# The values product of the first attention from rounded parts: the turned block copied by VectorE, rounded by ScalarE, its rest formed by GpSimd

## The chip, the cores and the metric

The kernel runs on one core of a Trainium2 chip. The metric is the device time of one execution in microseconds (us). Three runs of the kernel before took 2088.79, 2089.62 and 2090.61 us; the median is 2089.62 us. TensorE is PE in the profile, VectorE is DVE, ScalarE is ACT, GpSimd is POOL, and SyncE, which issues the weight loads, is SP.

## What is computed

The whole program is two transformer layers (an attention layer and a gated linear attention layer, each with an MLP) and a third layer with three mixers, for 512 tokens of width 1024. The change lies in the first layer's attention alone:

```python
s = jnp.einsum('bqhgd,bkhd->bhgqk', qblk, k, preferred_element_type=jnp.float32) * scale
p = jax.nn.softmax(s, axis=-1).astype(v.dtype)
return jnp.einsum('bhgqk,bkhd->bqhgd', p, v)
```

There are 16 query heads of width 64, 4 key/value heads, 512 tokens, no mask, float32 throughout.

## The kernel before

Activations lie transposed: 128 partitions are features, 512 columns are tokens. Almost every product is made from rounded parts. A float32 operand is split into `hi`, its value rounded to the type `float32r` (fp32r in the profile), and `lo`, the rest; `three` (lines 253 to 257) adds hi x hi, hi x lo and lo x hi into one PSUM bank by three matmuls. For weights ScalarE makes `w_hi` and VectorE `w_lo`.

The first attention (`attn_pe`, `attn_act`, `attn_dve`, `attn_pool`, lines 549 to 818) has two parts. First six blocks of the QKV projection are multiplied, while ScalarE and VectorE normalise and rotate queries and keys. Then comes a loop over `NU` = 64 units. Unit u is query tile u % 4 (128 queries) of head u // 4. Each engine has its own instruction queue, worked off in order, and its own loop over steps s; a unit passes through the engines with a fixed lag in steps, written out by hand:

- `scores(u)`, PE, step u: two matmuls against the keys' two parts, into bank 4 + u % 4.
- `top(u)`, DVE, step u + 2, for even u only: one reduction over the banks of units u and u + 1 gives both negated row maxima (`a_nmax`).
- `probs(u)`, ACT, step u + 2: exp of the scores with that bias, into one of four slots of `trow` (tile `sq`).
- `turn(u)`, PE, step u + 3: four 128x128 transposes into bank 2 + u % 2.
- `turned(u)`, DVE, step u + 4: one copy of that bank to `p_turned`, which holds two heads and lies where `h_hi` lies.
- `values(u)`, PE, step u + `A_LAG`, `A_LAG` = 8: one float32 matmul `a_v` x `p_turned`, accumulated over the four key chunks of head u // 4. The profile shows it as two records (x128 for 64). Half of `a_v`'s columns are ones, so that the product also gives the sum of the probabilities. The chunk 0 of a head waits for all four copies of the head.
- `inverse(h)`, ACT, once per head: logarithm and exp of the sums. `normed(h)`, DVE: multiply by it. `out_hi`, ACT, and the subtraction at line 818, POOL, once per two heads: the two parts of the output `a_q2` for the next projection.

Between these stand, once each, the rotation of the last query block (`evacuate`, `root`, `q_hi` on ACT; `cosine`, `sine`, `rotated`, `rooted`, `low` on DVE) and a weight block split in quarters. The output projection (`project`) follows: two of its eight row tiles at step 67, five behind the loop, the last in `pe_proj`.

The waits are on semaphores. The one that pairs DVE and ACT stands in `top` and `probs`:

```python
            def probs(u):
                act.wait_ge(a_top, u // 2 + 1)
                if u >= 4:
                    act.wait_ge(a_T, u - 3)
```

## Time and profile before

| | us |
|---|---|
| median of three runs (2088.79 to 2090.61) | 2089.62 |
| profiled execution, its time | 2088.29 |
| its span | 2086.6 |
| PE busy | 2029.9 (97%) |
| PE weight loads busy | 1629.5 (78%) |
| DVE busy | 1120.7 (54%) |
| ACT busy | 746.2 (36%) |
| POOL busy | 551.4 (26%) |

The profiled execution's own time is 1.7 us more than its span, and 1.3 us below the median of the runs. The attention loop lies between 94 and 216 us of the span. Rows of the timeline give the start of an instruction, its duration, engine, line, operation, names and shape. Durations of neighbours on one engine overlap a little, since an instruction starts before the record of the one ahead has ended; from start to start is what an engine needs for one.

### The profile page before, as it was taken

What the parts mean: (1) busy time and instruction counts of PE and PEld (TensorE: products, weight loads), DVE (VectorE), ACT (ScalarE), POOL (GpSimd) and SP (SyncE); (2) the same over time, 40 slices, a digit from 0 to 9 for tenths busy, and PEclk for the clock granted to TensorE, in tenths of its full rate; (3) what the DMA queues carried; (4) which work ended last, traced back from release to release, by engine and by line L of the source; (5) the groups of instructions that cost most, each with busy time, mean ns of one, the idle gap of its engine ahead of it and who ended that gap; (6) DMA issues with size and microseconds to landing.
All of it is one profiled execution on the core that took longest, in us unless ns stands there. A gap on an engine that the chain in (4) does not pass through costs nothing.

```text
span 2086.6 us, 23886 instructions
## 1 busy us (share of the span) xinstructions
PE 2029.9 (97%) x9416; PEld 1629.5 (78%) x9416; DVE 1120.7 (54%) x1127; ACT 746.2 (36%) x792; POOL 551.4 (26%) x497
## 2 busy tenths in 40 slices
PE   7999999999999998999999999999999989999996
PEld 5766778888877987778888888788988858888885
DVE  4697345455464435445555555783334464545455
ACT  5566332222234433322222234445553242222322
POOL 1100299990000000189991001423310000000000
PEclk9999999999999999999999999999999999999998
DMA  5400144433312220153442222232133312222221
GB/s 186 132 21 1 65 157 162 161 121 101 101 61 104 71 99 34 41 181 142 161 141 81 101 81 89 76 83 66 57 101 101 101 41 101 101 84 100 98 101 41
DMA packets 31773, 200.44 MB, mean 96 GB/s; under 512 B 3632, under 2 KB 3760, under 8 KB 8912
## 3 DMA queue, kind: packets, MB, share of 16 engines
q1 hardware_dynamic: 25552, 168.44, 23.5%
q0 software_dynamic: 6144, 30.94, 4.6%
q8 instruction: 53, 0.87, 0.2%
q14 instruction: 24, 0.20, 0.0%
HBM read 191.50 MB, written 2.10 MB: 93 GB/s over the span
## 4 chain that ended last, share of the span: by engine, by line
PE 95%; DVE 2%; ACT 2%; issue 1%; DMA 0%; DVEq 0%; SPq 0%; ACTq 0%
PE ps L255 26%; PE ps L257 26%; PE ps L256 25%; PE ps L612 3%; PE ps L367 2%; PE ps L599 1%; PE ps L1505 1%; PE ps L286 1%; PE ps L288 1%; PE ps L287 1%; PE ps L1050 1%; PE ps L1309 1%; PE ps L587 1%; PE ps L588 1%; PE ps L1489 1%
## 5 line engine op out<-in xcount | busy, mean ns | idle before, releaser
L217 ACT ACTIVATE w_hi<-w_raw 128x2048 fp32r<-128x2048 f32 x144 | 275.7, 1915 | 706.9 <-PE ps L257 706.7
L225 DVE TENSOR_TENSOR w_lo<-w_raw,w_hi 128x2048 fp32r<-128x2048 f32 x140 | 324.3, 2317 | 198.1 <-ACT w_hi L217 196.5
L255 PE MATMUL ps<-h_hi,w_hi 128*128 128x512 f32 x944 | 379.1, 402 | 7.9 <-DVE h_lo L419 4.0
L256 PE MATMUL ps<-h_lo,w_hi 128*128 128x512 f32 x944 | 371.1, 393 | 0.0
L257 PE MATMUL ps<-h_hi,w_lo 128*128 128x512 f32 x944 | 370.9, 393 | 0.0
L377 POOL TENSOR_TENSOR sq<-sq 128x1024 f32<-128x1024 f32 x9 | 31.6, 3509 | 879.4 <-ACT sq L351 729.4
L1293 POOL TENSOR_SCALAR ada_t<-ada_w,prm 128x256 f32<-128x256 f32 x192 | 220.2, 1147 | 9.9 <-DMA ada_w<-in_ada 9.0
L255 PEld LDWEIGHTS ps<-h_hi,w_hi 128*128 128x128 f32 x944 | 179.5, 190 | 51.5 <-issue 15.7
L257 PEld LDWEIGHTS ps<-h_hi,w_lo 128*128 128x128 f32 x944 | 179.1, 190 | 38.6
L256 PEld LDWEIGHTS ps<-h_lo,w_hi 128*128 128x128 f32 x944 | 179.4, 190 | 37.0 <-issue 1.4
L914 DVE TENSOR_TENSOR x<-x,ps 128x1024 f32<-128x1024 f32 x128 | 155.8, 1217 | 90.7 <-PE ps L257 90.7
L255 PE MATMUL ps<-m_xhi,w_hi 128*128 128x512 f32 x512 | 204.1, 399 | 0.0
L257 PE MATMUL ps<-m_hi,w_lo 128*128 128x512 f32 x512 | 203.0, 397 | 0.0
L257 PE MATMUL ps<-m_xhi,w_lo 128*128 128x512 f32 x512 | 203.0, 396 | 0.0
L255 PE MATMUL ps<-m_hi,w_hi 128*128 128x512 f32 x512 | 202.7, 396 | 0.0
L256 PE MATMUL ps<-m_xlo,w_hi 128*128 128x512 f32 x512 | 201.2, 393 | 0.0
L256 PE MATMUL ps<-m_lo,w_hi 128*128 128x512 f32 x512 | 201.2, 393 | 0.0
L1300 POOL TENSOR_TENSOR ada_acc<-ada_acc,ada_t 128x256 f32<-128x256 f32 x168 | 160.4, 954 | 14.0
L924 DVE SCALAR_TENSOR_TENSOR m_r<-ps,rstd 128x1024 f32<-128x1024 f32 x32 | 39.2, 1225 | 218.4 <-PE ps L257 218.4
L256 PEld LDWEIGHTS ps<-m_xlo,w_hi 128*128 128x128 f32 x512 | 96.2, 188 | 24.9 <-issue 1.0
L256 PEld LDWEIGHTS ps<-m_lo,w_hi 128*128 128x128 f32 x512 | 96.1, 188 | 23.9
L257 PEld LDWEIGHTS ps<-m_hi,w_lo 128*128 128x128 f32 x512 | 96.1, 188 | 23.5
(296 smaller groups left out, 3217.0 us busy)
## 6 DMA issues: line engine op xcount, KB each, us to landing
w_raw<-in_wb SPq DMA_DIRECT2D x154, 1024.0 KB, 4.9
ada_w<-in_ada POOLq DMA_DIRECT2D x24, 1024.0 KB, 5.4
a_sw<-a_g POOLq DMA_DIRECT2D x20, 128.0 KB, 2.8
x<-in_xT SPq DMA_DIRECT2D x4, 512.0 KB, 5.6
out_T<-x SPq DMA_DIRECT2D x4, 512.0 KB, 2.8
b_k<-b_k POOLq DMA_DIRECT2D x4, 256.0 KB, 5.4
b_kl<-b_kl POOLq DMA_DIRECT2D x4, 256.0 KB, 6.5
con<-in_con SPq DMA_DIRECT2D x1, 640.0 KB, 11.8
```

What stands on the lines that cost most here:

```text
L217: act.activation(w_hi[:, slot], w_raw[:, slot], ACT.Copy).then_inc(hi_done, 1)
L225: dve.tensor_tensor(w_lo[:, slot], w_raw[:, slot], w_hi[:, slot].bitcast(F32), ALU.subtract).then_inc(split_done, 1)
L255: pe.matmul(out, w[0], h[0], start=start, stop=False)
L256: pe.matmul(out, w[0], h[1], start=False, stop=False)
L257: return pe.matmul(out, w[1], h[0], start=False, stop=stop)
L367: last = pe.matmul(ps[:, bank, :], ones[:], squares(n)[:, slot, i * S:(i + 1) * S], start=(j == (2 if folded else 0) and i == 0), stop=(j ...
L377: pool.tensor_tensor(squares(n)[:, 0], squares(n)[:, 0], squares(n)[:, 1], ALU.add).then_inc(n_fold, 1)
L612: pe.matmul(ps[:, h % 2, :], at_["a_v"][:, c, kv, :], p_turned[:, half, :][:, c, :], start=c == 0, stop=c == TT - 1).then_inc(a_PV, 1)
L914: dve.tensor_tensor(xd, xd, pair_(2 + q % 2), ALU.add).then_inc(m_add, 1)
L924: dve.scalar_tensor_tensor(out=two(r), in0=pair_(par), scalar=0.0, in1=rstd[:].unsqueeze(1).to_broadcast([P, 2, S]), op0=ALU.max, op1=ALU. ...
L1293: pool.tensor_scalar(ml["ada_t"][:, k % 2], w, cact[:, k:k + 1], None, ALU.mult).then_inc(ada_row, 1)
L1300: ins = pool.tensor_tensor(acc, acc, ml["ada_t"][:, k % 2], ALU.add)
```

## The change

- The values are kept in two parts. ACT writes `a_vh` (`take_v`), DVE forms `a_vl` from PSUM and `a_vh` before the loop. POOL sets two tiles instead of one.
- `turned(u)` on DVE copies the bank to `a_p`, a float32 tile of two slots (`u % 2`). It waits until the subtraction of unit u - 2 has read the slot (`a_tl`).
- New on ACT: `rounded(u)`, step u + 5, behind `probs(u + 3)`. It rounds `a_p` to `p_hi`, which lies where `h_hi` lies.
- New on POOL: `lower(u)`, step u + 6. It writes `p_lo` = `a_p` - `p_hi`, where `h_lo` lies.
- `values(u)` on PE is `three` with the parts, in place of one float32 matmul, two steps later (`A_LAG` = 10). Chunk 0 waits for the four subtractions of its head.
- `inverse`, `out_hi` and `normed` move by two steps, `out_low` (before: line 818 in a loop of its own) stands between the subtractions.
- Room is made: the squares use `sq` and, for the last block, `a_sw`; `a_rot` has one slot, so `cosine` waits for `low` of the block ahead.

```diff
-            p_turned = sb("p_turned", [P, KT, S], F32, scope)
+            p_hi = sb("p_hi", [P, KT, S], F32R, scope)
+            p_lo = sb("p_lo", [P, KT, S], F32R, scope)
...
-                ("a_v", [P, TT, 4, P], F32), ("a_nmax", [P, 64], F32)]}
+                ("a_vh", [P, TT, 4, P], F32R), ("a_vl", [P, TT, 4, P], F32R), ("a_nmax", [P, 64], F32), ("a_inv", [P, S], F32)]}
             with ExitStack() as s2:
                 at_.update({n: sb(n, s, F32, s2) for n, s in [
-                    ("a_sq", [P, 1024]), ("a_g", [P, 2, 1024]), ("a_sw", [P, 2, 1024]), ("a_rot", [P, 2, 1024]), ("a_rs", [P, 1024]),
+                    ("a_g", [P, 2, 1024]), ("a_sw", [P, 2, 1024]), ("a_rot", [P, 1024]), ("a_rs", [P, 1024]),
                     ("a_cos", [P, S]), ("a_sin", [P, S])]})
             with ExitStack() as s2:
                 at_.update({n: sb(n, s, F32, s2) for n, s in [
-                    ("a_pad0", [P, 2, 1024]), ("a_o", [P, 2, S]), ("a_pad1", [P, 1024]), ("a_inv", [P, S])]})
+                    ("a_pad0", [P, 1024]), ("a_o", [P, 2, S]), ("a_pad1", [P, 1024]), ("a_p", [P, 2, S])]})
...
+        def squared(a):
+
+            return at_["a_sw"][:, 1] if a == LAST else sq[:, 0]
...
-        A_LAG = 8
+        A_LAG = 10
...
-                    pe.wait_ge(a_v_in, 2)
+                    pe.wait_ge(a_v_lo, 2)
...
+                    pe.wait_ge(a_v_lo, 2)
                 if c == 0:
-                    pe.wait_ge(a_pt, TT * h + TT)
+                    pe.wait_ge(a_tl, TT * h + TT)
                     if h >= 2:
                         pe.wait_ge(a_on, h - 1)
                 kv = 2 * (h // 8) + h % 2
                 half = slice(TT * (h % 2), TT * (h % 2) + TT)
-                pe.matmul(ps[:, h % 2, :], at_["a_v"][:, c, kv, :], p_turned[:, half, :][:, c, :], start=c == 0, stop=c == TT - 1).then_inc(a_PV, 1)
+                three(pe, ps[:, h % 2, :], (at_["a_vh"][:, c, kv, :], at_["a_vl"][:, c, kv, :]),
+                      (p_hi[:, half, :][:, c, :], p_lo[:, half, :][:, c, :]), c == 0, c == TT - 1).then_inc(a_PV, 1)
...
             def take_v():
                 act.wait_ge(block_done, B_QKV + V_BLOCK + 1)
-                act.wait_ge(a_vset, 1)
+                act.wait_ge(a_vset, 2)
                 for r in range(2):
-                    act.activation(v_heads("a_v", r), v_tokens(r), ACT.Copy).then_inc(a_v_in, 1)
+                    act.activation(v_heads("a_vh", r), v_tokens(r), ACT.Copy).then_inc(a_v_in, 1)
...
+            def rounded(u):
+                h, qt = divmod(u, TT)
+                act.wait_ge(a_pt, u + 1)
+                if qt == 0 and h >= 2:
+                    act.wait_ge(a_PV, TT * (h - 1))
+                half = slice(TT * (h % 2), TT * (h % 2) + TT)
+                act.activation(p_hi[:, half, qt * P:(qt + 1) * P], at_["a_p"][:, u % 2, :].rearrange("p (c q) -> p c q", q=P), ACT.Copy).then_inc(a_th, 1)
...
-            for s in range(NU + 11):
+            for s in range(NU + 13):
                 if 0 <= s - 2 < NU:
                     probs(s - 2)
+                if 0 <= s - 5 < NU:
+                    rounded(s - 5)
                 if s == 0:
                     evacuate(LAST)
                 if s == 4:
                     root(LAST)
                 if s == 14:
                     q_hi(LAST)
-                if s >= 12 and s % TT == 0:
-                    inverse((s - 12) // TT)
-                if s >= 18 and s % 8 == 2:
-                    out_hi((s - 18) // 8)
+                if s >= 14 and s % TT == 2:
+                    inverse((s - 14) // TT)
+                if s >= 20 and s % 8 == 4:
+                    out_hi((s - 20) // 8)
...
-                if a >= 2:
-                    dve.wait_ge(a_qhi, 2 * a - 2)
-                dve.tensor_tensor(two(at_["a_rot"][:, a % 2]), two(at_["a_g"][:, a % 2]), twice_row(at_["a_cos"][:]), ALU.mult)
+                if a >= 1:
+                    dve.wait_ge(a_ready, a)
...
+                if j == V_BLOCK:
+                    dve.wait_ge(a_vset, 2)
+                    for r in range(2):
+                        dve.wait_ge(a_v_in, r + 1)
+                        dve.tensor_tensor(v_heads("a_vl", r), v_tokens(r), v_heads("a_vh", r).bitcast(F32), ALU.subtract).then_inc(a_v_lo, 1)
...
             def turned(u):
-                h, qt = divmod(u, TT)
                 dve.wait_ge(a_T, u + 1)
-                if qt == 0 and h >= 2:
-                    dve.wait_ge(a_PV, TT * (h - 1))
-                half = slice(TT * (h % 2), TT * (h % 2) + TT)
-                dve.tensor_copy(p_turned[:, half, qt * P:(qt + 1) * P], ps[:, 2 + u % 2, :].rearrange("p (c q) -> p c q", q=P)).then_inc(a_pt, 1)
+                if u >= 2:
+                    dve.wait_ge(a_tl, u - 1)
+                dve.tensor_copy(at_["a_p"][:, u % 2, :], ps[:, 2 + u % 2, :]).then_inc(a_pt, 1)
...
-            for s in range(NU + 10):
+            for s in range(NU + 12):
                 if s >= 2 and s % 2 == 0 and s - 2 < NU:
                     top(s - 2)
                 if 0 <= s - 4 < NU:
                     turned(s - 4)
-                if s >= 13 and s % TT == 1:
-                    normed((s - 13) // TT)
+                if s >= 15 and s % TT == 3:
+                    normed((s - 15) // TT)
...
-            pool.memset(at_["a_v"][:], 1.0).then_inc(a_vset, 1)
+            for r in range(2):
+                pool.memset(at_["a_vh" if r == 0 else "a_vl"][:].bitcast(F32), 1.0 - r).then_inc(a_vset, 1)
...
-            for t in range(KT):
+            def lower(u):
+                h, qt = divmod(u, TT)
+                pool.wait_ge(a_th, u + 1)
+                half = slice(TT * (h % 2), TT * (h % 2) + TT)
+                w = slice(qt * P, (qt + 1) * P)
+                pool.tensor_tensor(p_lo[:, half, w], at_["a_p"][:, u % 2, :].rearrange("p (c q) -> p c q", q=P),
+                                   p_hi[:, half, w].bitcast(F32), ALU.subtract).then_inc(a_tl, 1)
+
+            def out_low(t):
                 pool.wait_ge(a_oh, t + 1)
                 pool.tensor_tensor(a_q2[:, t, 1, :], at_["a_o"][:, t % 2, :], a_q2[:, t, 0, :].bitcast(F32), ALU.subtract).then_inc(a_ol, 1)
+
+            for s in range(NU + 14):
+                if 0 <= s - 6 < NU:
+                    lower(s - 6)
+                if s >= 21 and s % 8 == 5:
+                    out_low((s - 21) // 8)
```

The order of instructions on ScalarE and VectorE around the ninth to twelfth unit. `sq<-ps,a_nmax` is the exp of a unit, `p_hi<-a_p` the new rounding, `a_inv` the inverse of a head's sums. ScalarE before:

```order
L677 ACTIVATE sq<-ps,a_nmax 128x512 [waits a_turned,a_max] x2
L655 ACTIVATE a_q2<-a_rot 64x2x512 [waits a_rows]
L655 ACTIVATE a_q2<-a_rot 64x2x512
L677 ACTIVATE sq<-ps,a_nmax 128x512 [waits a_turned,a_max] x2
L685 ACTIVATE a_inv<-ps 64x512 [waits a_pv]
L687 ACTIVATE a_inv<-a_inv 64x512 [waits a_ln]
L677 ACTIVATE sq<-ps,a_nmax 128x512 [waits a_turned,a_max] x2
L691 ACTIVATE a_q2<-a_o 128x512 [waits a_o_norm]
L677 ACTIVATE sq<-ps,a_nmax 128x512 [waits a_turned,a_max] x2
```

ScalarE now:

```order
L686 ACTIVATE sq<-ps,a_nmax 128x512 [waits a_turned,a_max]
L694 ACTIVATE p_hi<-a_p 128x4x128 [waits a_p_turned]
L686 ACTIVATE sq<-ps,a_nmax 128x512 [waits a_turned,a_max]
L694 ACTIVATE p_hi<-a_p 128x4x128 [waits a_p_turned]
L686 ACTIVATE sq<-ps,a_nmax 128x512 [waits a_turned,a_max]
L694 ACTIVATE p_hi<-a_p 128x4x128 [waits a_pv,a_p_turned]
L686 ACTIVATE sq<-ps,a_nmax 128x512 [waits a_turned,a_max]
L694 ACTIVATE p_hi<-a_p 128x4x128 [waits a_p_turned]
```

Every exp is now followed by a rounding of the unit three back, which waits for VectorE's copy; the exp ahead of it waits for the maximum (`a_max`), for every second unit a new one.

VectorE in the middle of the loop (`a_nmax<-ps` is the maximum for two units, `a_o` the normalisation of a head). Before:

```order
L759 TENSOR_REDUCE a_nmax<-ps 128x2 [waits a_scores]
L767 COPY p_turned<-ps 128x4x128 [waits a_turned] x2
L759 TENSOR_REDUCE a_nmax<-ps 128x2 [waits a_scores]
L767 COPY p_turned<-ps 128x4x128 [waits a_pv,a_turned]
L767 COPY p_turned<-ps 128x4x128 [waits a_turned]
L774 TENSOR_TENSOR a_o<-ps,a_inv 64x512 [waits a_o_lo,a_inv_s]
L759 TENSOR_REDUCE a_nmax<-ps 128x2 [waits a_scores]
```

VectorE now:

```order
L783 TENSOR_REDUCE a_nmax<-ps 128x2 [waits a_scores]
L789 COPY a_p<-ps 128x512 [waits a_p_lo,a_turned] x2
L783 TENSOR_REDUCE a_nmax<-ps 128x2 [waits a_scores]
L789 COPY a_p<-ps 128x512 [waits a_p_lo,a_turned] x2
L796 TENSOR_TENSOR a_o<-ps,a_inv 64x512 [waits a_o_lo,a_inv_s]
L783 TENSOR_REDUCE a_nmax<-ps 128x2 [waits a_scores]
L789 COPY a_p<-ps 128x512 [waits a_p_lo,a_turned] x2
```

The order is the same; each copy now also waits for GpSimd (`a_p_lo`), where before the first copy of a head waited for TensorE (`a_pv`).

GpSimd now, behind its transfers for the rotation (before, only the eight rows of `a_q2<-a_o,a_q2` stood here):

```order
L844 TENSOR_TENSOR p_lo<-a_p,p_hi 128x4x128 [waits a_p_hi] x16
L849 TENSOR_TENSOR a_q2<-a_o,a_q2 128x512 [waits a_o_hi]
L844 TENSOR_TENSOR p_lo<-a_p,p_hi 128x4x128 [waits a_p_hi] x8
L849 TENSOR_TENSOR a_q2<-a_o,a_q2 128x512 [waits a_o_hi]
L844 TENSOR_TENSOR p_lo<-a_p,p_hi 128x4x128 [waits a_p_hi] x8
L849 TENSOR_TENSOR a_q2<-a_o,a_q2 128x512 [waits a_o_hi]
```

The 64 subtractions of the blocks stand with the eight of the output in one queue; each waits for a rounding.

## Rows read from the trace of the kernel before

**Rows 1.** The page: the chain that ended last, by engine
```profile
PE 95%; DVE 2%; ACT 2%; issue 1%; DMA 0%; DVEq 0%; SPq 0%; ACTq 0%
```

**Rows 2.** Timeline of PE, one unit: start us, us, engine, line, names, idle before
```profile
150.02 0.60 PE L599 MATMUL ps<-identr,sq 128*128 128x128 f32 x4
...
150.92 1.02 PE L612 MATMUL ps<-p_turned,a_v 128*128 128x512 f32 x2
151.78 0.60 PE L599 MATMUL ps<-identr,sq 128*128 128x128 f32 x4
```

**Rows 3.** Timeline of PE, output projection behind the loop
```profile
217.39 0.40 PE L255 MATMUL ps<-a_q,w_hi 128*128 128x512 f32 x1
...
218.09 0.40 PE L255 MATMUL ps<-a_q,w_hi 128*128 128x512 f32 x1
```

**Rows 4.** Groups by line, 100 to 215 us: busy us, mean ns | idle before
```profile
L767 DVE COPY p_turned<-ps 128x512 f32<-128x512 f32 x64 | 43.5, 686 | 12.5 <-PE ps L599 12.4
...
L677 ACT ACTIVATE sq<-ps,a_nmax 128x512 f32<-128x512 f32 x62 | 41.6, 686 | 42.0 <-DVE a_nmax L759 41.7
...
L759 DVE TENSOR_REDUCE a_nmax<-ps 128x2 f32<-128x1024 f32 x31 | 37.6, 1214 | 2.7 <-PE ps L588 2.5
...
L687 ACT ACTIVATE a_inv<-a_inv 64x512 f32<-64x512 f32 x15 | 9.4, 630 | 0.5
...
L818 POOL TENSOR_TENSOR a_q<-a_o,a_q 128x512 fp32r<-128x512 f32 x7 | 9.2, 1311 | 101.9 <-ACT a_q L691 101.9
...
L685 ACT ACTIVATE a_inv<-ps 64x512 f32<-64x512 f32 x15 | 8.9, 593 | 4.4 <-PE ps L612 4.1
...
L655 ACT ACTIVATE a_q<-a_rot 64x1024 fp32r<-64x1024 f32 x2 | 2.1, 1050 | 0.0
```

**Rows 5.** Timelines of DVE, ACT and POOL, 152 to 155 us
```profile
152.10 1.22 DVE L759 TENSOR_REDUCE a_nmax<-ps 128x2 f32<-128x1024 f32 x1
...
153.36 0.69 ACT L677 ACTIVATE sq<-ps,a_nmax 128x512 f32<-128x512 f32 x1 [1.69 <-DVE a_nmax L759]
153.95 0.62 ACT L691 ACTIVATE a_q<-a_o 128x512 fp32r<-128x512 f32 x1
...
154.65 1.27 POOL L818 TENSOR_TENSOR a_q<-a_o,a_q 128x512 fp32r<-128x512 f32 x1 [11.66 <-ACT a_q L691]
...
154.17 0.69 DVE L767 COPY p_turned<-ps 128x512 f32<-128x512 f32 x1 [0.25 <-PE ps L599]
154.78 1.21 DVE L759 TENSOR_REDUCE a_nmax<-ps 128x2 f32<-128x1024 f32 x1
```

**Rows 6.** Timelines of ACT, DVE and PE: start, slope and end of the loop
```profile
103.22 1.25 ACT L677 ACTIVATE sq<-ps,a_nmax 128x512 f32<-128x512 f32 x2
...
105.25 1.21 DVE L759 TENSOR_REDUCE a_nmax<-ps 128x2 f32<-128x1024 f32 x1
...
158.42 0.68 DVE L774 TENSOR_TENSOR a_o<-ps,a_inv 64x512 f32<-64x512 f32 x1
159.03 1.21 DVE L759 TENSOR_REDUCE a_nmax<-ps 128x2 f32<-128x1024 f32 x1
...
204.06 1.22 DVE L759 TENSOR_REDUCE a_nmax<-ps 128x2 f32<-128x1024 f32 x1
...
215.59 0.80 PE L255 MATMUL ps<-a_q,w_hi 128*128 128x512 f32 x1
```

**Rows 7.** Timelines of POOL and DVE: subtractions beside VectorE's work
```profile
126.30 1.54 POOL L818 TENSOR_TENSOR a_q<-a_o,a_q 128x512 fp32r<-128x512 f32 x1 [27.35 <-ACT a_q L691]
...
208.74 1.29 POOL L818 TENSOR_TENSOR a_q<-a_o,a_q 128x512 fp32r<-128x512 f32 x1 [10.59 <-ACT a_q L691]
...
209.10 0.69 DVE L767 COPY p_turned<-ps 128x512 f32<-128x512 f32 x1 [0.38 <-PE ps L599]
```

**Rows 8.** Windows: PE, PEld, DVE, ACT, POOL busy, PEclk, DMA share, GB/s
```profile
790.00:800.00 10.00, 7.86 (x57) 7.89 (x58) 4.42 (x9) 0.00 (x0) 0.00 (x0) 0.83 0.32 107
...
1360.00:1370.00 10.00, 7.30 (x56) 6.69 (x55) 9.87 (x17) 3.37 (x4) 4.09 (x2) 1.00 0.47 130
```

More of the change, by code:

```diff
@@ L556, in aux @@
                 for i in range(2):
-                    last = pe.matmul(ps[:, (0 if a == LAST else 4) + i, :], mat(HALVES), at_["a_sq"][:, i * S:(i + 1) * S], start=True, stop=True)
+                    last = pe.matmul(ps[:, (0 if a == LAST else 4) + i, :], mat(HALVES), squared(a)[:, i * S:(i + 1) * S], start=True, stop=True)
                 last.then_inc(a_aux, 1)
@@ L654, in q_hi @@
                     dst = kv_heads("a_kh", r)[own[r]] if a == 0 else a_q2[own[r], 2 * a - 2:2 * a, r, :]
-                    act.activation(dst, two(at_["a_rot"][own[r], a % 2]), ACT.Copy).then_inc(a_qhi, 1)
+                    act.activation(dst, two(at_["a_rot"][own[r]]), ACT.Copy).then_inc(a_qhi, 1)
             def take_v():
                 act.wait_ge(block_done, B_QKV + V_BLOCK + 1)
-                act.wait_ge(a_vset, 1)
+                act.wait_ge(a_vset, 2)
                 for r in range(2):
-                    act.activation(v_heads("a_v", r), v_tokens(r), ACT.Copy).then_inc(a_v_in, 1)
+                    act.activation(v_heads("a_vh", r), v_tokens(r), ACT.Copy).then_inc(a_v_in, 1)
             for j in range(V_BLOCK):
@@ L713, in cosine @@
                     dve.wait_ge(rope_in, 32)
-                if a >= 2:
-                    dve.wait_ge(a_qhi, 2 * a - 2)
-                dve.tensor_tensor(two(at_["a_rot"][:, a % 2]), two(at_["a_g"][:, a % 2]), twice_row(at_["a_cos"][:]), ALU.mult)
+                if a >= 1:
+                    dve.wait_ge(a_ready, a)
+                dve.tensor_tensor(two(at_["a_rot"][:]), two(at_["a_g"][:, a % 2]), twice_row(at_["a_cos"][:]), ALU.mult)
             def sine(a):
@@ L723, in rotated @@
             def rotated(a):
-                rot = at_["a_rot"][:, a % 2]
+                rot = at_["a_rot"][:]
                 link(dve, dve.tensor_tensor(rot, rot, at_["a_sw"][:, a % 2], ALU.add))
             def rooted(a):
-                rot = at_["a_rot"][:, a % 2]
+                rot = at_["a_rot"][:]
                 dve.wait_ge(a_rs, a + 1)
@@ L736, in low @@
                 dve.wait_ge(a_qhi, 2 * a + r + 1)
-                rot = two(at_["a_rot"][own[r], a % 2])
+                rot = two(at_["a_rot"][own[r]])
                 if a == 0:
```

5 lines of the change are left out of this document (3 added, 2 removed).

## The prediction

> **What bounds the kernel now.** I read the page's chain first: 95% of it is PE [rows 1], so time is saved or lost where PE's work shrinks or where PE begins to wait. The change lies in the attention loop, so the timeline of PE there is next. One unit takes 151.78 - 150.02 = 1.76 us from transposes to transposes [rows 2]: 0.90 for four transposes and two score matmuls, 0.86 for the values product. PE has no gap in it. The groups of the stretch show what is beside it: ScalarE idles 42 us for the maxima, VectorE 12 us for the transposes, GpSimd nearly all the time [rows 4]. From the maximum of units 6 and 7 (105.25) to that of units 62 and 63 (204.06) 28 pairs of units take 98.8 us, 3.53 us each [rows 6]. The last values product ends about where the projection goes on, at 215.59.
>
> **What leaves PE.** The float32 product (0.86) becomes three matmuls of rounded parts. In the projection three such matmuls take 218.09 - 217.39 = 0.70 us [rows 3]. PE's unit would be 1.76 - 0.86 + 0.70 = 1.60 us. That alone is worth 64 x 0.16 = 10.2 us.
>
> **What the other engines get.** Taken by the load alone all of it fits nearly. ScalarE: exp 0.69, rounding 0.62 (the like copy of `a_o`, [rows 5]), a quarter of 0.59 + 0.63 [rows 4], an eighth of 0.62: 1.69 us a unit by durations, and about 0.1 less for each of its 2.6 instructions a unit by starts (an exp at 153.36, the next at 153.95, [rows 5]), so some 1.45. VectorE: half of 1.21, 0.69, a quarter of 0.69: 1.47. GpSimd: 1.27 [rows 5] and an eighth of it: 1.43. No one exceeds PE's 1.60.
>
> **But the order closes a ring.** `a_p` has two slots, so the copy of unit u waits for the subtraction of u - 2. Take an odd u. On VectorE the copy of u is followed at once by the maximum of units u + 3 and u + 4, with no wait for anybody. On ScalarE the rounding of u stands behind the exp of u + 3, and that exp needs this very maximum. So the rounding of u starts only when VectorE has copied u, reduced the next pair, and ScalarE has done the exp; then comes the subtraction, and only then may VectorE copy u + 2, with the next maximum behind it. One turn of the ring is two units:
>
> - maximum 1.22, handing over to ScalarE 0.04 (152.10 + 1.22 to 153.36), exp to next start 0.59, rounding 0.62, handing over to GpSimd 0.08 (153.95 + 0.62 to 154.65), copy to next start 0.61 (154.17 to 154.78), all from [rows 5];
> - the subtraction 1.27 to 1.29 without a disturbance [rows 5, 7], 1.54 at the worst, when one ran just behind VectorE's work on the last query block [rows 7]. I take 1.28, since in the ring VectorE's copies and maxima read PSUM, as they did in the undisturbed ones;
> - GpSimd to VectorE: no row shows it. Bounds are the two others, 0.04 and 0.08; I take 0.07.
>
> Sum 1.22 + 0.04 + 0.59 + 0.62 + 0.08 + 1.28 + 0.07 + 0.61 = **4.51 us** a pair, against 3.53 now. The even unit's copy, rounding and subtraction fit in between: its subtraction follows the odd one's on GpSimd and ends some 5.1 us after the maximum, while the even copy that needs it could start at 4.51 + 1.14, about 5.65.
>
> **The sum**, in the profiled execution:
>
> - 28 pairs x (4.51 - 3.53) = +27.5.
> - The normalisation of a head stands between an odd copy and the maximum, in the ring: 158.42 to 159.03 is 0.61 [rows 6]. 13 of them (heads 0 to 12) lie in the 28 pairs: +7.9. Of the four quarters of the weight block on VectorE two stand there as well, +1.2. The rotation of the last query block and the other quarters stand behind even copies, where VectorE has 4.51 - 2.4 = 2.1 us free: nothing; without that cover about 1.2 each.
> - At step 14 ScalarE does the two copies of the last query block (1.05 each, [rows 4]) and the first inverse (1.22) one after the other: the first normalisation, due 4.51 after the maximum, can start at 2.47 + 2.05 + 1.3 = 5.8: +1.3.
> - Start: the first rounding stands behind the exp of unit 3, at 103.22 + 0.59 = 103.81 [rows 6]; the first subtraction is done at 105.8, the copy of unit 2 and the cosine last until 107.65, the copy of unit 3 until 108.26. The maximum of 6 and 7 comes at 108.26 instead of 105.25: +3.0.
> - End: from the maximum of 62 and 63 the ring runs once more to the copy of unit 61 (3.90), its rounding and its subtraction (to 6.6); those of 62 and 63 follow one behind the other on GpSimd to about 9.8, then four products of 0.70 and 0.07, together 12.7. Before it was 215.59 - 204.06 = 11.5: +1.1. The output's last part (inverse, normalisation, rounding, subtraction, some 4.4 us) is hidden by 30 matmuls of the projection (7 us), as before.
> - Ahead of the loop VectorE gets two subtractions for the values' rest (some 0.7 each) and GpSimd a second fill. They lie in gaps before the first scores are reduced; nothing. If not covered, 1.3 us. The fill is at the very start, when GpSimd has nothing else. One slot of `a_rot` less makes VectorE wait for its own work: nothing.
> - PE's own saving of 10.2 is no term: PE waits in this loop now.
>
> 27.5 + 7.9 + 1.2 + 1.3 + 3.0 + 1.1 = 42.0. 2088.29 + 42.0 = 2130.3 for an execution like the profiled one, and the median of the runs lies 1.3 above it: **2131.6 us**. Behind the loop PE is the bound again and nothing is given back.
>
> **A rule against the trace.** A subtraction of GpSimd ran from 208.74 to 210.03, a copy of VectorE from PSUM from 209.10 to 209.79, both as long as ever [rows 7]. So I let the two run beside each other. The Trainium skill (SBUF — State Buffer, Terms) says that VectorE and GpSimd arbitrate for a shared port pair, exclusively, for a full instruction, and that the loser "fully blocks"; by that rule, taken by the letter for every write of VectorE, the time would be that of the third rival. The trace disagrees for such copies.
>
> **The rivals.**
>
> 1. *Faster: PE stays the bound.* The ring decides only above 2 x 1.60 = 3.2 us a pair. If the rounding of the odd unit did not wait behind the exp and the maximum, the two-slot buffer's own ring would be 0.69 + 0.04 + 0.62 + 0.08 + 1.28 + 0.07 = 2.8 us, below 3.2, and all other loads fit. Then 2089.6 - 10.2 = 2079.4. For it: no engine is loaded above 1.60 by starts. Against it: the order of the queues; ScalarE has idled for exactly these maxima [rows 4].
> 2. *No change: ScalarE's load decides.* If the order cost nothing, but its instructions took their full durations one after the other, 1.69 us a unit instead of 1.76: 2089.6 - 4 = about 2086.
> 3. *The subtraction excludes VectorE's copies.* The odd copy would wait until the even unit's subtraction has ended, 1.28 later in every turn: 31 x 1.28 = 40 more, 2172.
> 4. *PE's clock falls.* PE would be at work 3.2 of 4.8 us. At 790 the granted clock was 0.83, that is partly the lower of its two levels (1.2 and 2.4 GHz), after gaps of PE; at 1360, with PE busy 7.30 of 10 us, it was 1.00 [rows 8]. At the lower level a pair would take PE 6.4 us instead of 4.8: 28 x 1.6 = 45 more, 2177; half of the time, 2154. The gaps here are short ones, below 1.5 us, so I hold it unlikely.
>
> That the change does not do what it says can hardly be: the parts are of the kind that the scores use, three matmuls for one.
>
> **How the numbers follow.** Forecast 0.80, rival 1 0.05, rival 2 0.04, rival 3 0.05, rival 4 0.06. Bounds of the forecast: the subtraction at 1.54 adds 0.26 x 28 = 7.3, longer handing over 0.05 x 2 x 28 = 2.8; the normalisations hidden would take off 7.9, the step 14 term 1.3, and a shorter handing over 0.8. So 2121.5 to 2141.7; toward rival 4 I go up to 2150, down to 2119, which leaves out rivals 1, 2, 3 and half of 4, 0.17, and a little of the forecast. A measurement of this kernel tells about 0.2% (4 us) from no change. Faster by more: rival 1 and a part of 2, 0.06. Within it: 0.03. Slower: 0.91.
>
> **What would show it.** In the profile after, the maxima stand 4.5 us apart, 5.1 with a normalisation between; ScalarE's rounding of odd units starts right behind the exp; GpSimd's subtraction is 1.28 us, and the odd copy on VectorE is released by it; PE shows some 30% idle from 105 to 250, released by VectorE's and ScalarE's work; the projection goes on near 257.6. The forecast is wrong if the maxima come at 3.2 us (rival 1), if the odd copy waits for the even unit's subtraction (3), or if the granted clock is below 1.00 there (4). A subtraction of another length moves the time by 28 times the difference.

## The result, and the profile of the changed kernel

| | before | changed |
|---|---|---|
| median of the runs, us | 2089.2 (4 runs, 2087.99 to 2090.61) | 2138.84 (4 runs, 2136.70 to 2141.37) |
| profiled execution, us | 2088.29 | 2136.7 |
| its span, us | 2086.6 | 2134.9 |

The ratio is 1.0236, with a 95% interval of 1.022 to 1.0252: slower by 2.4%. The profiled executions lie 48.4 us apart; the forecast had 42.0. The single runs of the changed kernel stand at 2136.70 twice, 2140.98 and 2141.37. The two longer ones show a mean granted clock of 0.983, the shorter ones 0.987 and 0.986. Later runs of the kernel before lie as far apart (2087 to 2095 us, with 0.989 to 0.986). What parts them was not looked into, and the working below goes by the profiled executions.

The page of the changed kernel: the engines, PE's busy tenths in 40 slices, and the chain that ended last by engine, the answer to [rows 1].

```profile
PE 2037.5 (95%) x9480; PEld 1639.5 (77%) x9480; DVE 1125.8 (53%) x1129; ACT 779.5 (37%) x856; POOL 638.7 (30%) x562
PE   8977799999999999899999999999999989999997
...
PE 88%; DVE 5%; ACT 3%; POOL 2%; issue 2%; DMA 0%; DVEq 0%; SPq 0%; ACTq 0%
```

PE is still busy 95% of the span, but its share of the chain fell from 95% to 88%. In its place stand VectorE, ScalarE and GpSimd. In three of PE's 40 slices (107 to 267 us) it is busy seven tenths; before, PE was busy 108.7 of the 109 us from 107 to 216.

The groups of 100 to 255 us, the answer to [rows 4] (line, engine, operation, names, shapes, count, then busy us, mean ns, idle before in us and what ended it):

```profile
L844 POOL TENSOR_TENSOR p_lo<-a_p,p_hi 128x512 fp32r<-128x512 f32 x60 | 79.9, 1337 | 69.1 <-ACT p_hi L694 69.0
L686 ACT ACTIVATE sq<-ps,a_nmax 128x512 f32<-128x512 f32 x62 | 42.4, 684 | 58.6 <-DVE a_nmax L783 58.3
L789 DVE COPY a_p<-ps 128x512 f32<-128x512 f32 x61 | 41.8, 687 | 55.1 <-POOL p_lo L844 54.9
L606 PE MATMUL ps<-identr,sq 128*128 128x128 f32 x248 | 41.3, 291 | 32.7 <-ACT sq L686 17.5 <-DVE a_p L789 15.2
L694 ACT ACTIVATE p_hi<-a_p 128x512 fp32r<-128x512 f32 x61 | 37.9, 622 | 0.0
```

Each engine waits for another one: ScalarE 58 us for maxima, VectorE 55 us for GpSimd's subtractions, GpSimd 69 us for ScalarE's rounded parts, and PE for two of them. Before, VectorE waited only for PE's transposes [rows 4]. The rounding itself never waits in this stretch (0.0): it always stands behind an exp.

One turn of this, from maximum to maximum, from the timelines of three engines (start us, us, engine, line, names, and in brackets the idle time and its end):

```profile
161.58 0.69 DVE L789 COPY a_p<-ps 128x512 f32<-128x512 f32 x1 [2.12 <-POOL p_lo L844]
162.30 0.69 DVE L796 TENSOR_TENSOR a_o<-ps,a_inv 64x512 f32<-64x512 f32 x1
163.03 1.23 DVE L783 TENSOR_REDUCE a_nmax<-ps 128x2 f32<-128x1024 f32 x1
...
164.29 0.69 ACT L686 ACTIVATE sq<-ps,a_nmax 128x512 f32<-128x512 f32 x1 [1.68 <-DVE a_nmax L783]
164.87 0.62 ACT L694 ACTIVATE p_hi<-a_p 128x512 fp32r<-128x512 f32 x1
...
165.57 1.27 POOL L844 TENSOR_TENSOR p_lo<-a_p,p_hi 128x512 fp32r<-128x512 f32 x1 [1.59 <-ACT p_hi L694]
...
166.95 0.69 DVE L789 COPY a_p<-ps 128x512 f32<-128x512 f32 x1 [2.10 <-POOL p_lo L844]
167.56 1.22 DVE L783 TENSOR_REDUCE a_nmax<-ps 128x2 f32<-128x1024 f32 x1
```

From 163.03 to 167.56 it is 4.53 us: 1.26 to the exp, 0.58 to the rounding, 0.70 to the subtraction, 1.38 to the copy, 0.61 to the next maximum. These are the steps that the forecast named, in its order, at 4.51. The turn ahead of it holds a normalisation (162.30) and took 5.38 from 157.65 to 163.03. Of the maxima, units 6 and 7 came at 108.70, units 22 and 23 at 153.14, units 62 and 63 at 251.41, and the projection went on at 264.32:

```profile
108.70 1.21 DVE L783 TENSOR_REDUCE a_nmax<-ps 128x2 f32<-128x1024 f32 x1
...
153.14 1.21 DVE L783 TENSOR_REDUCE a_nmax<-ps 128x2 f32<-128x1024 f32 x1
```
```profile
264.32 0.40 PE L256 MATMUL ps<-a_q,w_hi 128*128 128x512 f32 x1
```

### The profile page after: what moved, and what is told of

It is laid out like the page before. It is cut to its first block, busy times and chain, and to the rows that moved or that the text cites. A ratio compares the mean times of both kernels' runs of the same rounds, so it can differ in the third digit from the quotient of the medians.

```text
span 2134.9 us, 24207 instructions
## 1 busy us (share of the span) xinstructions
PE 2037.5 (95%) x9480; PEld 1639.5 (77%) x9480; DVE 1125.8 (53%) x1129; ACT 779.5 (37%) x856; POOL 638.7 (30%) x562
## 4 chain that ended last, share of the span: by engine, by line
PE 88%; DVE 5%; ACT 3%; POOL 2%; issue 2%; DMA 0%; DVEq 0%; SPq 0%; ACTq 0%
PE ps L258 25%; PE ps L256 25%; PE ps L257 25%; PE ps L368 2%; POOL p_lo L844 2%; DVE a_p L789 1%; PE ps L1542 1%; PE ps L287 1%; PE ps L289 1%; PE ps L288 1%; DVE a_nmax L783 1%; ACT p_hi L694 1%; PE ps L1087 1%; PE ps L1346 1%; PE ps L1526 1%
## 5 line engine op out<-in xcount | busy, mean ns | idle before, releaser
L961 DVE SCALAR_TENSOR_TENSOR m_r<-ps,rstd 128x1024 f32<-128x1024 f32 x32 | 39.2, 1225 | 218.1 <-PE ps L258 218.1
L256 PEld LDWEIGHTS ps<-m_xhi,w_hi 128*128 128x128 f32 x512 | 96.1, 188 | 23.5 <-issue 1.0
```

What stands on the lines that cost most here:

```text
L256: pe.matmul(out, w[0], h[0], start=start, stop=False)
L961: dve.scalar_tensor_tensor(out=two(r), in0=pair_(par), scalar=0.0, in1=rstd[:].unsqueeze(1).to_broadcast([P, 2, S]), op0=ALU.max, op1=ALU. ...
```

## The experiments

My theory: the order of the queues, with a buffer of two slots, closes a ring through three engines, and nothing else matters while it does. The rivals that the result left: PE (three matmuls, a clock that falls), ScalarE's load, GpSimd's load, GpSimd and VectorE blocking each other. Each edit is against the changed kernel unless another is named. "Maxima" is the mean distance between two pairs of units behind units 22 and 23 (from the maximum of 22 and 23 to that of 62 and 63, through 20; before it was 3.44: 135.20 to 204.06). Each ratio is to runs of the kernel before that were made beside it; their medians lie between 2089.0 and 2090.3.

| run | what is different | median us (range) | ratio to before, 95% | maxima us |
|---|---|---|---|---|
| changed kernel | | 2138.84 (2136.70 to 2141.37) | 1.0236 (1.022 to 1.0252) | 4.91 |
| e2_one_product | one matmul for three in the values product | 2137.64 (2135.82 to 2138.42) | 1.0231 (1.0214 to 1.0248) | 4.91 |
| e3_subtract_twice | each subtraction twice | 2188.65 (2187.33 to 2190.47) | 1.0475 (1.0457 to 1.0492) | 6.40 |
| e7_norm_even | normalisation behind even copies | 2129.27 (2128.66 to 2130.61) | 1.0185 (1.0166 to 1.0204) | 4.53 |
| e1_round_first | rounding ahead of the exp | 2102.01 (2101.25 to 2102.75) | 1.0058 (1.0041 to 1.0075) | 3.60 |
| e4_three_slots | three slots for the copies | 2103.24 (2101.85 to 2103.68) | 1.0063 (1.0046 to 1.008) | 3.64 |
| e5_three_slots_round_first | both | 2096.10 (2094.58 to 2099.02, 9 runs) | 1.0027 (1.0016 to 1.0038) | 3.37 |
| e14_spread_only | other work spread out | 2133.36 (2133.16 to 2135.56) | 1.0211 (1.0195 to 1.0226) | 4.95 |
| e13_spread_both | e5 and other work spread out | 2097.03 (2095.51 to 2098.20, 6 runs) | 1.0033 (1.0021 to 1.0045) | 3.71 |
| e6_from_psum | no copy, no GpSimd: both parts from PSUM | 2126.98 (2125.58 to 2128.39) | 1.0174 (1.0154 to 1.0194) | 4.60 |
| e8_lag9 | e6, product a step earlier, maximum first | 2101.23 (2099.36 to 2101.58) | 1.005 (1.0033 to 1.0068) | 3.72 |
| e9_lag8 | e8, product another step earlier | 2111.21 (2110.32 to 2114.48) | 1.0105 (1.0085 to 1.0124) | 4.06 |
| e10_lag9_rest_first | e6, product a step earlier | 2106.08 (one run) | none (one run) | 3.93 |

### Is PE the bound?

```diff
-                three(pe, ps[:, h % 2, :], (at_["a_vh"][:, c, kv, :], at_["a_vl"][:, c, kv, :]),
-                      (p_hi[:, half, :][:, c, :], p_lo[:, half, :][:, c, :]), c == 0, c == TT - 1).then_inc(a_PV, 1)
+                pe.matmul(ps[:, h % 2, :], at_["a_vh"][:, c, kv, :], p_hi[:, half, :][:, c, :], start=c == 0, stop=c == TT - 1).then_inc(a_PV, 1)
```

This kernel leaves out the two products with a rest; copies, roundings and subtractions stay.

> The values product is one matmul of the two rounded parts instead of three (the two products with a rest are left out), all of ScalarE, VectorE and GpSimd is as in the change. PE loses 128 matmuls, 30 us of work. Theory A (ring): PE waits in the loop anyway, only the last four units' products count, 4 x 0.47 = 2 us less, and 2 to 3 more for what stands at step 67: 2133 to 2138. Theory B' (PE's work or its lower clock is still part of the bound): 10 to 30 us less, 2108 to 2128.

128 matmuls less (two of three, 64 units), some 30 us of PE's work by a third of the 0.70 of [rows 3] each, changed the time by 1 us of 2138, inside the spread. The granted clock tells more. Windows of this kernel and of the changed one (stretch: us, busy us and count of PE, PEld, DVE, ACT, POOL, then the granted clock):

```profile
160.00:180.00 20.00, 13.67 (x62) 8.72 (x60) 11.33 (x14) 12.72 (x23) 11.72 (x10) 0.91 0.00 0
220.00:240.00 20.00, 13.69 (x56) 8.97 (x56) 11.66 (x15) 12.73 (x23) 11.38 (x9) 0.83 0.00 0
```
```profile
108.00:112.00 4.00, 3.82 (x13) 2.52 (x13) 3.64 (x5) 2.06 (x4) 2.08 (x2) 0.50 0.00 0
...
128.00:136.00 8.00, 5.80 (x24) 4.25 (x25) 6.20 (x6) 4.35 (x8) 4.76 (x3) 0.79 0.00 1
160.00:180.00 20.00, 15.04 (x76) 10.19 (x75) 11.32 (x14) 12.70 (x23) 11.61 (x10) 1.00 0.01 1
```

In the kernel with one product the clock was 0.91 and 0.83, partly at the lower level of 1.2 GHz, with the maxima as far apart (4.91) and the same time. PE waits here, and a slower PE waits less.

### Is it the ring?

Three edits change the ring: one makes it longer, two cut it at different places.

```diff
+                pool.tensor_tensor(p_lo[:, half, w], at_["a_p"][:, u % 2, :].rearrange("p (c q) -> p c q", q=P),
+                                   p_hi[:, half, w].bitcast(F32), ALU.subtract).then_inc(a_twice, 1)
+                pool.wait_ge(a_twice, u + 1)
```

These lines stand ahead of the subtraction of the changed kernel, which still raises `a_tl` and gives the same values once more.

> GpSimd forms each rest twice, one after the other; 64 subtractions of 1.28 us more. Theory A (ring): each turn, that is each pair of units, takes 1.3 us more, since one subtraction per turn lies in it and the even unit's stands in its slack: 31 x 1.3 = 40 us more, about 2178; the even one may add up to 10. Theory B (GpSimd's load): 64 x (2 x 1.28 + 0.16) = 174 us for the loop against 156 now, 18 to 20 us more, about 2158. If GpSimd is not in the chain at all: no change.

It came 49.8 us later than the changed kernel, at the upper end of the ring's forecast and far above the load theory's. A pair without a normalisation took 5.85, that is 1.32 more than 4.53: one further subtraction and its wait (on GpSimd, 187.02 to 188.36 is 1.34). VectorE's wait for GpSimd, from the waits of 110 to 210 us (us, times, longest), in the changed kernel and then here. The longest grew from 2.1 to 3.4, by one subtraction:

```profile
DVE a_p L789 <- POOL p_lo L844: 34.1, 22, 2.1
...
DVE a_p L790 <- POOL p_lo L848: 41.2, 24, 3.4
```

The first cut changes ScalarE's order:

```diff
+                if 0 <= s - 5 < NU:
+                    rounded(s - 5)
                 if 0 <= s - 2 < NU:
                     probs(s - 2)
-                if 0 <= s - 5 < NU:
-                    rounded(s - 5)
```

> ScalarE's two instructions of a step change places: the rounding of unit u now stands ahead of the exp of unit u + 3, nothing else is changed. Theory A (the ring through maximum, exp, rounding and subtraction sets the pace): the ring is cut, what is left of it is 0.69 + 0.04 + 0.62 + 0.08 + 1.28 + 0.07 = 2.8 us a pair, below PE's 3.2; a pair takes 3.2 to 3.5 us instead of 4.51, the time falls by 45 to 60 us to 2080 to 2092. Theory B (the added load of ScalarE and GpSimd sets the pace, whatever the order): no change, 2135 to 2142. Theory C (PE's lower clock after its gaps costs most of the loss): part of it remains, 2110 to 2130.

The second gives the copies a third slot, in a buffer (`rstd`) that the loop does not use otherwise:

```diff
+        def slot(u):
+            return rstd[:] if u % 3 == 2 else at_["a_p"][:, u % 3, :]
-                if u >= 2:
-                    dve.wait_ge(a_tl, u - 1)
+                if u >= 3:
+                    dve.wait_ge(a_tl, u - 2)
```

> The copied block gets a third slot (in the unused rstd), VectorE's copy waits for the subtraction of u - 3; the orders of all engines stay. Theory A (ring over two slots): from an odd unit the ring now leads to the even unit u + 3, in whose place VectorE has slack, so a turn covers four units: about 4.5 + 1.8 us for four units, below PE's 6.4; the time is 2080 to 2095. Theory B (load of the engines): no change, 2135 to 2142.

Either edit alone gives back some 36 of the 50 us, without taking an instruction away. So the ring is shown as the cause of most of the loss: to swap two instructions or to add one slot is worth three quarters of it. Both missed theory A's ranges, by 10 and by 8 us, so something else is left. Both together:

> Three slots and the rounding ahead of the exp together. If what is left over the kernel before (13 to 14 us in each of the two alone) is a second ring through the slots or the order, it falls too: 2083 to 2092. If it is the start of the loop (the rotation of the last query block and the quarters, beside GpSimd) together with the loads of ScalarE, it stays: 2096 to 2103.

It is the best version of the study and still 0.27% slower than the kernel before, with an interval that excludes 1. Of the expectation's two answers it meets the second, at its lower edge (2096). The maxima say where the loss is. From units 22 and 23 to 62 and 63 it takes 67.3 us, 1.5 us less than the 68.9 before: there, with little other work in the loop, the shorter product of PE does bring a little. But the first maximum of the count, of units 6 and 7, is 2.1 us later (107.38), and the 8 pairs with the other work in them take 36.7 us instead of 29.95. Windows of the two stretches in this kernel:

```profile
107.00:144.00 37.00, 29.36 (x152) 20.81 (x151) 33.90 (x37) 28.44 (x47) 27.13 (x20) 1.00 0.00 1
144.00:211.00 67.00, 64.20 (x351) 50.40 (x350) 54.51 (x71) 60.45 (x103) 55.66 (x44) 1.00 0.05 17
```

In the first VectorE is busy 33.9 of 37 us (92%), in the second ScalarE 60.5 and PE 64.2 of 67 (90% and 96%). Before, ScalarE had idled 42 us for maxima [rows 4] and the other work had room there. PE's 1.60 us a unit (3.2 a pair) is missed by 0.17 a pair in the second stretch. The chain of waits has this piece there once in two heads, from 160.20, from 173.79 and from 187.38 (start us, us, what):

```profile
173.79 0.48 ACT sq L690
174.27 0.09 issue
174.36 0.62 ACT p_hi L698
174.98 0.58 ACT sq L690
175.58 0.60 ACT a_inv L706
176.21 0.64 ACT a_inv L708
176.90 0.69 issue
177.59 1.22 DVE a_nmax L787
```

Exp, rounding, exp and both parts of an inverse on ScalarE, a normalisation (it runs in the 0.69 of `issue`), a maximum, and the next exps wait for that. In the other head of the two the chain holds the inverse as well, then PE (171.33 to 173.17) and a rounding that waits for PE's product, since it overwrites what this product reads; such waits are short (2.6 us in 4 waits from 144 to 211). The two heads take 13.59 us, 3.40 a pair. The inverse stands ahead of a normalisation, and this ahead of a maximum: behind the first ring there is a second one. No kernel was run that moves the inverse, so that it is this order, and not the load of 90% and more on ScalarE and PE, stays argued.

### What the normalisation costs

```diff
-                if s >= 15 and s % TT == 3:
-                    normed((s - 15) // TT)
+                if s >= 16 and s % TT == 0:
+                    normed((s - 16) // TT)
```

The rounding and the subtraction of the heads' output follow one step later as well.

> The change as it is, but VectorE normalises a head behind the copy of an even unit, one step later, and not behind that of an odd one (the output's two parts follow by one step). Theory A says that 13 normalisations of 0.73 to 0.87 us stood in the ring, and that behind an even copy VectorE has about 2 us free: 9 to 11 us less, 2127 to 2130. If they are not in the ring, no change: 2136 to 2141.

All pairs of the later stretch are 4.53 us apart now, and the 20 pairs take 90.6 us, 7.7 less than the 98.3 of the changed kernel. So a normalisation in the ring costs 0.77 (ten of them), where I had 0.61. The medians lie 9.6 us apart, 0.74 for each of 13; the profiled executions lie 7.8 apart. Where it comes from stands in the timeline above: 161.58 to 162.30 is 0.72 and 162.30 to 163.03 is 0.73, though a copy directly ahead of a maximum takes 0.61 (166.95 to 167.56). The distance ahead of the normalisation is 0.72 or 0.73 in all ten; the one behind it is 0.73 and 0.61 by turns, which makes turns of 5.38 and 5.24. At 0.72 the next instruction starts when the record of the one ahead has ended, at 0.61 some 0.1 before; why was not tried. The kernel before shows it too (157.69 to 158.42 ahead of [rows 6]'s normalisation); I had read only the second distance, 158.42 to 159.03.

### What crowded the start

Beside the units the loop has other work: sine, rotation, root, copies and subtractions for the last query block, and the quarters of a weight block. All of it lies in steps 6 to 23. In e14 it is spread over steps 10 to 64; two places of the edit:

```diff
-                if s == 14:
-                    q_hi(LAST)
+                if s in (24, 32):
+                    q_hi(LAST, ((s - 24) // 8,))
...
-                if 20 <= s < 24:
-                    quarter_lo(dve, B_WO0 + 1, (B_WO0 + 1) % 2, s - 20)
+                if 52 <= s < 68 and s % 4 == 0:
+                    quarter_lo(dve, B_WO0 + 1, (B_WO0 + 1) % 2, (s - 52) // 4)
```

> The same spreading in the change itself, two slots and the exp first; all moved instructions stand behind even copies, where the ring leaves VectorE and ScalarE about 2 us. The change's trace from the maximum of 6 and 7 to that of 22 and 23 took 44.4 us where the ring's 8 x 4.51 and three normalisations of 0.8 make 38.5. If this excess of 6 is crowding at step 14 and VectorE and GpSimd in each other's way, most of it goes, less what GpSimd still loses beside the ten moved ones: 2132 to 2136. If not: 2137 to 2141.

> Three slots and the rounding first, and besides the rotation of the last query block, its two copies on ScalarE and the quarters of the weight block no longer crowd steps 4 to 23 but stand four or eight steps apart up to step 64 (nothing of them is needed before unit 48 or the output projection). Without this the eight pairs from the maximum of units 6 and 7 took 36.7 us, against 30.0 before the change and 27.2 in the same run's own later stretch. If crowding (and GpSimd beside VectorE's work from SBUF) is what costs there, 5 to 8 us go: 2088 to 2092, about even with the kernel before. If it is the added load, wherever it stands: 2094 to 2097.

In the changed kernel itself it gave 5.5 us by the medians, as expected, and 3.3 between the profiled executions: the stretch from units 6 and 7 to 22 and 23 shrank from 44.4 to 39.2 us, and the 20 later pairs grew from 98.3 to 99.0. On top of e5 it gave nothing (2097.03 against 2096.10), which is the expectation's second answer. There the crowded stretch shrank from 36.7 to 27.2 us, and the 20 later pairs grew from 67.3 to 74.3: 28 pairs at 3.37 would be 94.4 us, e5 took 104.1 and e13 101.4. With VectorE, ScalarE and PE near their limit the other work costs 7 to 10 us wherever it stands. The 2.6 us that e13 is ahead in these pairs do not show in its time. What the crowding is, the changed kernel's timelines show:

```profile
107.40 1.91 POOL L844 TENSOR_TENSOR p_lo<-a_p,p_hi 128x512 fp32r<-128x512 f32 x1 [0.31 <-ACT p_hi L694]
...
151.34 1.33 POOL L844 TENSOR_TENSOR p_lo<-a_p,p_hi 128x512 fp32r<-128x512 f32 x1 [1.23 <-ACT p_hi L694]
...
151.42 1.79 DVE L242 TENSOR_TENSOR w_lo<-w_raw,w_hi 128x512 fp32r<-128x512 f32 x1
```
```profile
132.04 3.48 POOL L844 TENSOR_TENSOR p_lo<-a_p,p_hi 128x512 fp32r<-128x512 f32 x2 [0.58 <-ACT p_hi L694]
...
132.29 2.11 DVE L761 TENSOR_TENSOR a_q<-a_rot,a_q 64x1024 fp32r<-64x1024 f32 x1
```

A subtraction of GpSimd takes 1.28 alone; beside the rotation (106.69 to 108.18) it took 1.91, and two of them 3.48 beside the subtraction for the queries. VectorE's quarter took 1.79 and the one of the queries 2.11; in e14, where each of them started ahead of GpSimd's subtraction, their means are 0.69 and 1.21. All these VectorE instructions read two operands from SBUF. The quarter had started 0.08 behind GpSimd's subtraction and ended at 153.21, 0.54 after the subtraction of GpSimd (152.67), nearly its own length: it did not share, it stood until the other had ended. That is the rule which the forecast had weighed (SBUF — State Buffer, Terms, in the Trainium skill), and for this instruction the trace agrees, with 1.79. The copy from PSUM at 166.95 ran 0.69 and the maximum at 167.56 ran 1.22, with an instruction of GpSimd from 166.80 to 168.09 beside them. So it is all through the loop: 19 copies, 28 maxima and 4 normalisations overlap GpSimd's work by more than 0.3 us, and none took over 0.69, 1.23 and 0.69. The Trainium skill (GPSIMD Engine Reference, 1. Specifications) puts the contention exactly so: with VectorE instructions in a 2-port mode "or with two SBUF inputs". The trace agrees for two SBUF inputs (1.79 against 0.68), and no run here bears on the 2-port mode.

### A version without the copy

If the ring needs the copy, leave it out: ScalarE rounds straight from PSUM, VectorE forms the rest from PSUM, GpSimd has nothing to do, and PE's turn waits until both have read.

```diff
+                act.wait_ge(a_T, u + 1)
+                act.activation(p_hi[:, half, qt * P:(qt + 1) * P], ps[:, 2 + u % 2, :].rearrange("p (c q) -> p c q", q=P), ACT.Copy).then_inc(a_th, 1)
...
-                dve.tensor_copy(at_["a_p"][:, u % 2, :], ps[:, 2 + u % 2, :]).then_inc(a_pt, 1)
+                dve.tensor_tensor(p_lo[:, half, w], ps[:, 2 + u % 2, :].rearrange("p (c q) -> p c q", q=P),
+                                  p_hi[:, half, w].bitcast(F32), ALU.subtract).then_inc(a_tl, 1)
```

The rounding stands ahead of the exp at step u + 4, the rest ahead of the maximum at step u + 5; `A_LAG` stays 10.

> The copy and GpSimd's subtraction are gone: ScalarE rounds the turned block straight from PSUM, ahead of the exp, and VectorE forms the rest from PSUM and the rounded part, one instruction of 0.69 in place of its copy. PE then waits for this rest before it fills the bank again: 0.69 + 0.62 + four transposes and hand-overs, some 2.0 us a pair plus what stands ahead on PE, 1.2: at most 3.2. Theory A: every ring is at or below PE's 3.2 us a pair, so the loop takes 6 to 10 us less than before the change: 2079 to 2086, faster than both kernels. Theory B (ScalarE's load, 1.45 to 1.69 a unit): 2088 to 2095.

It missed by 40 us. The waits of 110 to 210 us name what I had overlooked: `p_hi` has two halves, one for each head, and the rounding of head h must wait until the values product of head h - 2 is done. The rounding had moved a step ahead, the product had not.

```profile
ACT p_hi L694 <- PE ps L258: 23.4, 10, 3.2
```
```profile
157.14 0.60 ACT L694 ACTIVATE p_hi<-ps 128x512 fp32r<-128x512 f32 x1 [2.15 <-PE ps L258]
...
166.56 0.60 ACT L694 ACTIVATE p_hi<-ps 128x512 fp32r<-128x512 f32 x1 [2.18 <-PE ps L258]
```

Once a head of four units (9.42 us here) ScalarE stands still for 2.15 us. Three follow-ups move the product (`A_LAG` 9 or 8) and change the order of maximum and rest:

> As the kernel with the rounding from PSUM, with two edits: the values product runs 9 steps behind (not 10), and VectorE's maximum stands ahead of the rest again. The trace of the run with 10 steps shows ScalarE's rounding of a head's first unit waiting for the values product of two heads before (31.6 us in 14 waits), because its place is in the half of p_hi that this product still reads. With 9 steps that product stands one step earlier on PE: the waits go, and every ring is at or below PE's 3.2 us a pair: 2080 to 2090. If the wait is not the cause: 2120 to 2127.

> The same with 8 steps. The values product of a head's first chunk then comes in the step in which VectorE forms the rest of its last chunk, so PE waits for VectorE once a head: 16 x 0.5 to 1 us more than with 9 steps, 2088 to 2100. If it is as fast as with 9 steps, PE is far enough behind not to feel it.

> 9 steps, but the rest stands ahead of the maximum on VectorE. Then rounding of an odd unit, rest, maximum, exp and the next odd rounding are a ring of 0.66 + 0.65 + 1.25 + 0.59 = 3.15 us a pair, about PE's own 3.2: within 5 us of the order with the maximum first. If the order of VectorE was the cause of the loss with 10 steps: 2115 to 2127.

At lag 9 25.8 us came back with the maximum first (e8), and 20.9 with e6's own order (e10, one run), so that wait was most of the loss. It is not gone: from 110 to 210 us it is still 10.2 us in 12 waits, against e6's 23.4 in 10. At lag 8 PE waits for the rest (17.4 us in 110 to 210) and 10 us are lost again. The order of maximum and rest is worth under 5 us, by one run. But e8 and e9 both end 11 us above what I had expected, and e8's chain shows the second ring too, with the rest and PE in it:

```profile
161.35 0.68 ACT sq L686
162.05 0.60 ACT a_inv L702
162.68 0.64 ACT a_inv L704
163.34 0.69 DVE a_o L798
164.06 1.22 DVE a_nmax L783
165.31 0.70 DVE p_lo L790
166.15 0.63 PE ps L606 x4
...
167.94 0.45 PE ps L606 x4
...
168.91 0.68 ACT sq L686
```

Exp, two parts of the inverse, normalisation, maximum, rest; then on PE the transposes, two scores, three products and the next transposes (166.15 to 168.39), a rounding, and the next head's exp 7.56 us after the first. The head behind it takes 7.32, and the two together make 3.72 a pair, e8's pace. Two kernels with different parts thus end in the same place: the inverse and the normalisation in line with a maximum. That this order costs the time is read from the chains and not shown by a run.

## Why the prediction was right, and where it was off

**The sign and the mechanism were right.** The ring, its five steps, its length (4.51 against 4.53), the wait that ends last (the odd copy on VectorE, released by GpSimd) and the absence of a gain from PE's shorter product stood as forecast. e3 makes the ring longer by what one more subtraction costs, e1 and e4 cut it at two places and get 36 us back, e2 shows that PE is no bound. The time lies inside the range of 2119 to 2150, 7.2 us above the point. That it lies below 2141.7 is in part luck: this margin was made of a longer subtraction in every turn (7.3) and longer handing over (2.8), and of these only 0.04 us a turn of handing over came in every turn. Crowding and normalisations filled the rest.

**Where the other 6.4 us of the profiled execution came from** (48.4 against 42.0), by the maxima:

| stretch | forecast | measured | step |
|---|---|---|---|
| maximum of units 6 and 7 | 108.26 | 108.70 | +0.4: the cosine took 1.49 beside a subtraction |
| to units 22 and 23, 8 pairs | 40.4 | 44.4 | +4.0: crowding 3.4, the rest turns and normalisations |
| to units 62 and 63, 20 pairs | 96.3 | 98.3 | +2.0: normalisations 1.6, turns 0.4 |
| to the projection | 12.7 | 12.9 | +0.2 |

- *28 pairs, +27.5.* Right: 4.53 for 4.51, at 28 pairs 0.6 us. The subtraction stayed at 1.28; the hand-over from GpSimd to VectorE, which no row had shown, is 0.11 (165.57 + 1.27 to 166.95), not 0.07.
- *13 normalisations, +7.9.* The term was mis-sized: 0.61 each was the distance behind the normalisation, and the one ahead of it is 0.1 longer. In the 20 later pairs 98.3 - 20 x 4.53 = 7.7 for ten of them, 0.77; e7, which takes them out of the ring, gives the same.
- *Other work behind even copies, nothing.* This step failed. I had compared its duration with 2.1 us of free time of VectorE. But such an instruction reads two operands from SBUF, draws out GpSimd's subtraction (two took 3.48 for 2.56) and is drawn out itself (0.69 to 1.79). Where the rotation stood in a turn with two subtractions, the turn took 4.78 to 4.83; in e14, without it, 4.51. The subtraction is in the ring, so cover on VectorE did not help. Beyond the 1.2 that I had given two of the quarters it made 3.4 us in the 8 pairs, and 0.3 at the start, where the cosine took 1.49 for 1.21. e14 took 5.2 out of the 8 pairs, the step 14 term and the priced quarters among them. My upper bound for the subtraction, 1.54, was too low: 1.91 was seen here and 2.28 in e5. The 1.54 had been a sign of the same thing, misread: that subtraction (from 126.30) did not run just behind VectorE's work but beside its end, as VectorE's row of the kernel before shows, from 125.49 to 126.70. The first row here is this one, the second the cosine of the changed kernel:

```profile
125.49 1.21 DVE L742 TENSOR_TENSOR a_q<-a_rot,a_q 64x1024 fp32r<-64x1024 f32 x1
```
```profile
106.69 1.49 DVE L735 TENSOR_TENSOR a_rot<-a_g,a_cos 128x1024 f32<-128x1024 f32 x1
```

- *Step 14, +1.3.* Right: the turn took 6.40, forecast 4.51 + 0.61 + 1.3 = 6.42. On ScalarE, the two copies, the inverse and then VectorE's normalisation:

```profile
125.47 2.13 ACT L664 ACTIVATE a_q<-a_rot 64x1024 fp32r<-64x1024 f32 x2
127.62 0.59 ACT L702 ACTIVATE a_inv<-ps 64x512 f32<-64x512 f32 x1
128.25 0.63 ACT L704 ACTIVATE a_inv<-a_inv 64x512 f32<-64x512 f32 x1
...
128.91 0.68 DVE L796 TENSOR_TENSOR a_o<-ps,a_inv 64x512 f32<-64x512 f32 x1 [1.18 <-ACT a_inv L704]
129.52 1.20 DVE L783 TENSOR_REDUCE a_nmax<-ps 128x2 f32<-128x1024 f32 x1
```

- *End, +1.1, and what lies ahead of the loop, nothing.* Right within 0.2 us.

**The rivals.** *PE stays the bound* and *ScalarE's load decides* were false for the changed kernel. The first also gave a size: if the order cost nothing, 2079.4. That size is false as well. With the ring cut in both ways the time is 2096.10, since PE's 1.60 us were not reached and the other work had no room left: against 0.32 less a pair than before, e5 is 2.1 us behind at the first maximum of the count, loses 9.3 in the 8 pairs and 4.9 in the 20 later ones. The step that failed is "no engine is loaded above 1.60 by starts" as a reason for a pace of 1.60. For that the loads of three engines would all have to fit without a gap, and the other work would have to find room; ScalarE's by my own count was 1.45, and e5's windows show it busy 60.45 of 67 us at 1.68 a unit, 1.52. *The subtraction excludes VectorE's copies* was false for copies and maxima from PSUM, as [rows 7] had shown. It was true for instructions with two operands in SBUF, which I had not told apart. *PE's clock falls* did happen, to 0.50 from 108 to 112 and 0.79 from 128 to 136, and cost nothing that the trace shows: the chain of what ended last holds no piece of PE from 100 to 152 us. Two of PE's gaps ahead of the fall, 1.56 and 1.63 us, were longer than the 1.5 that I had gone by. My price (PE's work at half speed in place of the ring) took the fall for lasting. It lasted a few turns, and from 128 to 136 PE had gaps to spare (5.80 busy of 8); e2 shows the same pace at 0.83 and 0.91 with less work for PE.

## What to carry to other kernels

Before adding a pass over another engine, follow one buffer slot round: which instruction frees it, what stands ahead of that in each in-order queue, and whether that again needs the slot; the sum of the steps is the pace, however low each engine's load. A third slot, or the other order of two lines, gave back 36 of 50 us here. When the first ring is cut look for the second before you count on the load bound, and give a GpSimd instruction in a ring its longest duration when VectorE works beside it on two operands from SBUF.
